# Token block 0 of a two-block layer stack goes ahead from the cross attention to its first expert head

## What is computed

```
h = h + concat([hm, ha]) @ w_out
h = h + memory_cross_attention(rmsnorm(h, g_cross), ...)      # 4 heads of 256, 256 memory rows
xn = rmsnorm(h, g_ffn)
per block of 128 tokens, per head (8 heads), per token:
    q1, q2 = halves of (xn @ w_pq)[head];  s1 = q1 . sub_keys1, s2 = q2 . sub_keys2   # 128 each
    v1, i1 = top_k(s1, 16);  v2, i2 = top_k(s2, 16)
    top_s, pos = top_k(v1[:, None] + v2[None, :], 16);  e = 128 * i1 + i2 at pos
    coef = softmax(top_s) * gelu(expert_down[e] . xn)          # 16 experts
    out += sum over the 16 of coef * expert_up[e]
out = rmsnorm(h + out, g_final)
```

## Time and profile before

| | |
|---|---|
| median of 3 runs | 1639.43 us (1639.33 to 1641.08) |
| profiled execution | 1639.54 us, span 1637.8 us |
| busy: PE, DVE, ACT, POOL | 81%, 59%, 21%, 30% |
| chain that ended last | PE 53%, DMA 26%, DVE 12%, POOL 4% |
| first gather issued | 954.24 us from the span's start |

### The profile page before, as it was taken

How to read it: one execution, slowest core, us unless ns; L and a number is a source line. 1 busy time by engine, 2 the same in 40 slices (tenths; PEclk the granted TensorE clock), 3 DMA queues, 4 the chain that set the end, 5 groups by cost and what they waited for, 6 DMA issues and landing times.

```text
span 1637.8 us, 14570 instructions
## 1 busy us (share of the span) xinstructions
PE 1332.4 (81%) x5214; PEld 936.5 (57%) x5214; DVE 959.0 (59%) x1851; ACT 338.5 (21%) x677; POOL 493.6 (30%) x390
## 2 busy tenths in 40 slices
PE   7999999999999999999999987565566656555554
PEld 5665668888888888886787776222222222222221
DVE  7799974123311000323412168898988998988977
ACT  2444222321100000122312122111111121111111
POOL 2477670000000000000000024755555555555550
PEclk9999999999999999999999998877777777877776
DMA  6222222244344444322242377999999999999995
GB/s 238 77 78 77 78 103 103 103 157 177 128 149 148 150 145 153 128 103 103 77 143 91 117 303 288 405 422 421 422 422 421 422 422 421 422 422 422 421 422 211
DMA packets 55150, 389.75 MB, mean 238 GB/s; under 512 B 6336, under 2 KB 6656, under 8 KB 8368
## 3 DMA queue, kind: packets, MB, share of 16 engines
q0 software_dynamic: 37488, 271.20, 40.1%
...
q10 hardware_dynamic: 1040, 2.26, 0.4%
...
## 4 chain that ended last, share of the span: by engine, by line
PE 53%; DMA 26%; DVE 12%; POOL 4%; issue 2%; ACT 2%; ACTq 0%; DVEq 0%
DMA feat<-in_expert,arena 26%; PE psD L930 16%; PE psD L978 7%; PE psD L384 7%; PE psD L881 6%; POOL feat L1782 4%; PE psD L949 3%; PE psD L1288 1%; DVE feat L1795 1%; PE psN L313 1%; DVE arena L619 1%; DVE feat L1829 1%; DVE feat L537 1%; PE psD L874 1%; PE psD L575 1%
## 5 line engine op out<-in xcount | busy, mean ns | idle before, releaser
L930 PE MATMUL psD<-feat,ring 128*128 128x256 f32 (+1 forms) x1248 | 278.1, 383 | 4.4 <-DVE feat L338 3.2
L930 PEld LDWEIGHTS psD<-feat,ring 128*128 128x128 f32 x1248 | 238.6, 192 | 39.1 <-issue 4.5
L1782 POOL DMA_INDIRECT arena<-in_expert,arena x102 | 140.0, 1373 | 208.7 <-DVE arena L1762 53.0
L1970 POOL DMA_DIRECT2D arena<-in_sub x1 | 0.6, 577 | 525.2 <-ACT feat L1504 525.2
L881 PE MATMUL psD<-feat,ring 128*128 128x256 f32 (+1 forms) x576 | 138.1, 396 | 3.0 <-ACT feat L916 3.0
L1795 DVE CUSTOM_DVE_ANT_0 arena<-arena,feat 128x1024 f32<-128x1024 f32 x102 | 120.7, 1220 | 12.8 <-DMA arena<-in_expert,arena 12.8
L881 PEld LDWEIGHTS psD<-feat,ring 128*128 128x128 f32 x576 | 109.2, 194 | 30.5 <-issue 10.5
L1619 PE MATMUL psB<-arena 128*128 128x512 f32 x96 | 73.2, 923 | 64.1 <-ACT arena L1694 64.1
L1782 POOL DMA_INDIRECT feat<-in_expert,arena x77 | 107.7, 1398 | 57.9 <-DVE feat L1829 17.0
L978 PE MATMUL psD<-feat,ring 128*128 128x256 f32 x512 | 111.2, 379 | 0.0
L384 PE MATMUL psD<-feat,ring 128*128 128x256 f32 x512 | 110.8, 379 | 0.0
...
## 6 DMA issues: line engine op xcount, KB each, us to landing
ring<-in_w SPq DMA_DIRECT2D x108, 1024.0 KB, 4.8
arena<-in_expert,arena POOLq DMA_INDIRECT x102, 27.1
feat<-in_expert,arena POOLq DMA_INDIRECT x77, 28.7
...
arena<-in_w_akv POOLq DMA_DIRECT2D x1, 1024.0 KB, 5.2
feat<-in_memT POOLq DMA_DIRECT2D x1, 1024.0 KB, 5.9
...
ring<-in_expert,arena POOLq DMA_INDIRECT x60, 28.7
```

The costliest lines, as they stand in the source:

```text
L930: mm = nc.tensor.matmul(psD[:, 2 * (c % 2) + m, 0:T], ring[:, c % RING, k, m * P:(m + 1) * P], x[:, k], start=(k == 0), stop=(k == KT - 1))
L1782: (nc.gpsimd.indirect_dma_start(GPAIR[b], None, a["expert"], bass.IndirectOffsetOnAxis(ap=EID[:, t, c:c + 1], axis=0)) .then_inc(s_gb[b], 16))
```

## The change

1. **Sums of squares (norms 2 to 6).** VectorE adds tiles 2, 3 and 4, 5 onto tiles 0, 1 (`squares_dve`); TensorE then has four calls of sums, all after the last chunk or in the middle of the next one, where it had eight.
2. **Cross attention by pairs.** Heads go two at a time for a token block; the scores of a head stand behind the next query chunk.
3. **The output projection is token-major and goes by token block**, adding onto the residual that TensorE puts into PSUM first. ScalarE copies the sum out, squares it and takes the root. Only the gain is applied before the query; the reciprocal root scales the scores and the copy of xn afterwards. Norm 7's own sums are gone.
4. **Block 0 goes ahead**: projection, turn, head 0's queries and scores, and the route come before block 1's. Head 0's query weights are a load of their own (`pq0`) into the room of the squares; the stream has 107 chunks. The residual starts off the accumulator, so TensorE's residual matmuls of the experts go.
5. **Buffers and waits.** `SOON` becomes a list that says which of the sixteen buffers round 0 uses; `LATEWAIT` says what frees each of the others. Buffer 3 (`pq0`'s room) waits for the queries of both blocks.
6. **Order.** The first gelu stands before the seven remaining query chunks, the others behind chunks 1, 4 and 6 of them. Round 1's route comes after round 0's second step instead of before its first; from there the route of a round ends in step 1 of the round before it, half a round later than it did. In the last round `both` comes one step earlier, behind q = 1.

```diff
-SOON = 9
+SOON = [4, 5, 6, 9, 10, 11, 12, 0, 3]
...
-          ("aq", 2), ("mv", 2), ("xva", 3), ("w_out_2", 4), ("xvb", 1), ("xq", 4), ("xo", 4), ("pq", 8)]
+          ("aq", 2), ("mv", 2), ("xva", 3), ("w_out_2", 4), ("xvb", 1), ("xq", 4), ("xo", 4), ("pq", 7)]
...
-    def sums_pe(i, j):
-        nc.tensor.wait_ge(s_sqp, 4 * (i - 2) + j + 1)
-        if j == 0:
-            nc.tensor.wait_ge(s_rt, i)
-        for k in (2 * j, 2 * j + 1):
-            mm = nc.tensor.matmul(psN[:, 0:T2], ones[:, :], SQ[:, k, 0:T2], start=(k == 0), stop=(k == KT - 1))
-        if j == 3:
...
+    def squares_dve(i, link):
+        for j in (1, 2):
+            nc.vector.wait_ge(s_sqp, 4 * (i - 2) + j + 1)
+            ins = nc.vector.tensor_tensor(SQ[:, 0:2, 0:T2], SQ[:, 0:2, 0:T2], SQ[:, 2 * j:2 * j + 2, 0:T2], ALU.add)
+            if j == 1:
+                link(ins)
+        ins.then_inc(s_sqa, 1)
+
+    def sums_pe(i):
+        nc.tensor.wait_ge(s_rt, i)
+        nc.tensor.wait_ge(s_sqa, i - 1)
+        for k in (0, 1, 6, 7):
+            if k == 6:
+                nc.tensor.wait_ge(s_sqp, 4 * (i - 2) + 4)
+            mm = nc.tensor.matmul(psN[:, 0:T2], ones[:, :], SQ[:, k, 0:T2], start=(k == 0), stop=(k == 7))
+        mm.then_inc(s_ms, 1)
...
+    late = {1: slot(feat[:, 3]), 2: slot(ring[:, 3]), 7: slot(ring[:, 0]), 8: slot(ring[:, 1]), 13: slot(ring[:, 2]),
+            14: slot(XN), 15: slot(feat[:, 4])}
+    GPAIR = [soon[SOON.index(i)] if i in SOON else late[i] for i in range(PTOP)]
+    XP = soon[3].rearrange("p (n h s) -> p n h s", n=4, h=2)
+    XPT = soon[4].rearrange("p (n b t) -> p n b t", n=4, b=4)
...
+    def project_pe(t, js, ks):
+        for j in js:
+            c = FIRST["xo"] + j
+            for k in ks:
+                if t == 0 and k == 0:
+                    nc.tensor.wait_ge(s_w[c % RING], (c // RING + 1) * 16)
+                if j == js[0] and k % 4 == 0:
+                    nc.tensor.wait_ge(s_xoc, 2 * t + k // 4 + 1)
+                mm = nc.tensor.matmul(XSUM[t, j // 2][:, (j % 2) * CW:(j % 2) * CW + CW], OX[:, k, blk(t)],
+                                      ring[:, c % RING, k, :], start=False, stop=True, skip_group_check=True)
+            if t:
+                mm.then_inc(s_chunk, 1)
+        if ks[-1] == KT - 1 and js[-1] % 2:
+            mm.then_inc(s_h3, 1) if t == 0 else None
...
+    def blocks_pe():
+        for j in range(4):
+            chunk_pe(FIRST["xq"], j, XN2, T2, fresh=5 if j == 0 else None)
+            if j:
+                cross_scores_pe(j - 1)
+        cross_scores_pe(3)
+        residual_pe(0)
+        cross_turn_pe(0, 0)
+        cross_turn_pe(1, 0)
+        cross_out_pe(0, 0)
+        cross_turn_pe(0, 1)
+        project_pe(0, (0, 1), range(4))
+        cross_out_pe(0, 1)
+        project_pe(0, (2, 3), range(4))
+        project_pe(0, (0, 1), range(4, 8))
+        project_pe(0, (2, 3), range(4, 8))
+        hturn_pe(0, 0)
+        cross_turn_pe(1, 1)
+        hturn_pe(0, 1)
+        nc.tensor.wait_ge(s_sk, 64)
+        query0_pe(0, 0)
+        query0_pe(0, 1)
+        score0_pe(0, 0)
+        cross_out_pe(1, 0)
+        score0_pe(0, 1)
+        xturn_pe(0)
+        cross_out_pe(1, 1)
+        residual_pe(1)
+        project_pe(1, (0, 1), range(8))
+        project_pe(1, (2, 3), range(8))
+        hturn_pe(1, 0)
+        hturn_pe(1, 1)
+        query0_pe(1, 0)
+        query0_pe(1, 1)
+        xturn_pe(1)
+        score0_pe(1, 0)
+        score0_pe(1, 1)
...
+    def blocks_dve(link):
+        for t in range(2):
+            cross_peak_dve(t, 0, link)
+        for t in range(2):
+            cross_share_dve(t, 0, link)
+        for t in range(2):
+            cross_peak_dve(t, 1, link)
+        cross_share_dve(0, 1, link)
+        cross_turned_dve(0, 0)
+        cross_share_dve(1, 1, link)
+        cross_turned_dve(1, 0)
+        cross_turned_dve(0, 1)
+        gains_dve(0)
+        cross_turned_dve(1, 1)
+        gains_dve(1)
+        rstd_dve(0)
...
+    def state_act(t, b):
+        if t:
+            nc.scalar.wait_ge(s_chunk, FIRST["xo"] + 2 * b + 2)
+        else:
+            nc.scalar.wait_ge(s_h3, b + 1)
+        nc.scalar.activation(ACC[:, t, 512 * b:512 * b + 512], XSUM[t, b], ACT.Identity).then_inc(s_acc, 1)
+        if b:
+            nc.scalar.wait_ge(s_acc, 2 * t + 2)
+            nc.scalar.activation(XTOK[:, t], ACC[:, t], ACT.Square, accum_out=F7[:, t, 0:1]).then_inc(s_fsq, 1)
+            nc.scalar.wait_ge(s_fsq, t + 1)
+            (nc.scalar.activation(F7[:, t, 1:2], F7[:, t, 0:1], ACT.Sqrt, bias=epsc[:, 0:1], scale=1.0 / D)
+             .then_inc(s_frt, 1))
...
+    def blocks_act(first_gelu):
+        for j in range(3):
+            pair_act(FIRST["xq"], j, QX[:, 2 * j:2 * j + 2])
+        for t in range(2):
+            cross_exp_act(t, 0)
+        pair_act(FIRST["xq"], 3, QX[:, 6:8])
+        for t in range(2):
+            cross_exp_act(t, 1)
+        nc.scalar.activation(F7[:, 1, 3:4], epsc[:, 0:1], ACT.Sqrt)
+        cross_out_act(0, 0)
+        cross_out_act(0, 1)
+        state_act(0, 0)
+        state_act(0, 1)
+        query0_act(0, 0)
+        query0_act(0, 1)
+        score0_act(0, 0)
+        cross_out_act(1, 0)
+        score0_act(0, 1)
+        xturn_act(0)
+        cross_out_act(1, 1)
+        state_act(1, 0)
+        state_act(1, 1)
+        for b in range(2):
+            nc.scalar.wait_ge(s_ht, 3 + b)
+            for i in range(4):
+                k = 4 * b + i
+                ins = nc.scalar.activation(XN2[:, k, P:T2], HTURN[1, b][:, i * P:(i + 1) * P], ACT.Identity,
+                                           scale=col("g_ffn_2", k))
+            ins.then_inc(s_xh, 1)
+        for m in range(2):
+            query0_act(1, m)
+        first_gelu()
...
     def pair(g, i):
-        return i % SOON if g == 0 else i
+
+        return SOON[i % len(SOON)] if g == 0 else i
...
+        def queries(h):
+            if h == 2:
+                nc.tensor.wait_ge(s_psc, 4)
+            chunk_pe(FIRST["pq"], h - 1, XN2, T2, clear=FIRST["xq"] + 2 + h,
+                     mid=(lambda: scores(h - 1)) if h > 1 else None)
...
-            nc.scalar.wait_ge(s_ps, h + 2)
-            (nc.scalar.activation(SCO[:, :, 2 * h:2 * h + 2], psB[:, h % 2].rearrange("p (t x n) -> p t x n", t=2, x=2),
-                                  ACT.Identity).then_inc(s_psc, 1))
-            if h in (3, 5, 6, 7):
-                coefficients(0, (3, 5, 6, 7).index(h))
+            pair_act(FIRST["pq"], h - 1, QH[:, 2 * h:2 * h + 2])
+            if h > 1:
+                scored(h - 1)
+            if h in (1, 4, 6):
+                coefficients(0, (h + 1) // 2)
+        scored(PH - 1)
...
 
+
...
-
+        last = {}
         for g in range(2 * PH):
             t, h = g // PH, g % PH
             nc.gpsimd.wait_ge(s_eid, g + 1)
             for i in range(PTOP):
                 b = pair(g, i)
-                if g == 0 and i >= SOON:
-                    nc.gpsimd.wait_ge(*used(0, i - SOON))
-                if g == 1 and i < SOON:
-                    nc.gpsimd.wait_ge(*used(0, i + SOON if i + SOON < PTOP else i))
-                if g == 1 and i == SOON:
-                    nc.gpsimd.wait_ge(s_ps, PH + 1)
-                if g > 1:
-                    nc.gpsimd.wait_ge(*used(g - 1, i))
+                if b in last:
+                    nc.gpsimd.wait_ge(*used(*last[b]))
+                elif b == 3:
+                    nc.gpsimd.wait_ge(s_qh, 4)
+                elif g == 0 and i == 0:
+                    nc.gpsimd.wait_ge(s_xo, 4)
+                elif b in LATEWAIT:
+                    nc.gpsimd.wait_ge(*LATEWAIT[b])
+                last[b] = g, i
                 c = h * PTOP + i
...
+    def routes(g, q):
+
+        if g == 0 and q < 2:
+            return []
+        h, part = (g + 1, q + 2) if q < 2 else (g + 2, q - 2)
+        return [(h, part)] if h < 2 * PH else []
...
                 dve.scalar_tensor_tensor(out=ACC[:, t, v], in0=ACC[:, t, v], scalar=FS[:, t, 2:3], in1=GFIN[:, v],
                                          op0=ALU.mult, op1=ALU.mult).then_inc(s_done, 1)
-        for g in range(2):
-            for part in range(4):
-                route_dve(g, part, link)
+        for part in range(4):
+            route_dve(0, part, link)
         for g in range(2 * PH):
             for q in range(len(steps(g))):
                 if g % PH == 0 and q == 0:
                     dve.wait_ge(s_ttc, 2 * (g // PH) + 2)
                 down_dve(g, q)
-                if g + 2 < 2 * PH:
-                    route_dve(g + 2, q, link)
+                if g == q == 0:
+                    rstd_dve(1)
+                for h, part in routes(g, q):
+                    route_dve(h, part, link)
                 if g == 2 * PH - 1 and q == 3:
                     close(1)
                 coef_dve(g, q, link)
                 up_dve(g, q)
+                if g == 0 and q == 1:
+                    for part in range(4):
```

(6 more changed lines are left out.)

362 lines of the change are left out of this document (185 added, 177 removed).

## The result

| | before | after |
|---|---|---|
| median, us | 1639.62 (1639.33 to 1641.08, 4 runs) | 1603.74 (1593.06 to 1609.08, 4 runs) |
| ratio to before | | 0.9766 (95%: 0.974 to 0.9793) |
| profiled execution / its span | 1639.54 / 1637.8 | 1593.06 / 1591.3 |
| first gather | 954.24 | 912.35 |
| first gather to the end of the span | 683.6 | 679.0 |

The change makes the kernel 2.3% faster. Its single times were 1593.06, 1609.08, 1599.22 and 1608.27 us: the profiled execution lies 1.3 us from the predicted 1594.4, and two of the others lie 15 to 16 us above it. The kernel before stays within 2 us. Both facts need an explanation.

The account below looks back on a forecast made before the run. DMA bounds the expert stage, TensorE what precedes it. First gather 912.6 + 1.8 + 653.6 + 2.6 + 0.2 = 1570.8; span 1592.6, forecast 1594 us, 45 faster (chance 0.68, alone 1587 to 1602); range 1586 to 1611.

Parts of the forecast that it names:

- rival 3: Norms 2 to 6: the sums save nothing because VectorE's additions come too late; 9.3 us less gain, 1604 us; chance 0.05.
- the sums of squares: Norms 2 to 6: fewer TensorE calls save 1.73 us each, 2.42 for norm 4, together 9.3 us.
- rival 4: Steady rounds: later addresses let the queue run dry in all 14; at 4 us a round 56 us, 1651; chance 0.03.
- The path of block 0: From the four cross-query chunks to the first gather: 72.2 us instead of 104.5, first gather at 912.6.
- Rival 2: On block 0's path TensorE's clock falls to 1.2 GHz; first gather 21 us later, 1615 us; chance 0.06.
- The four more loads: After the first gather seven query chunks load instead of three: 263 units, four more, costing 9.9 us.
- the slow engine: Expert stage: one DMA engine falls back 0.04 us a unit; 0.2 us for the four more units.
- The start: After the first gather the DMA queue never runs dry; 2.6 us lost, where the kernel before lost 15.2.
- rival 1: After the first gather the start starves as before: 15.2 us lost instead of 2.6, 1607 us; chance 0.14.
- The late addresses: Steady rounds: addresses come half a round later, yet nothing runs dry and rounds stay 40.4 us apart.
- the end: Last round: `both`, 1.23 us, moves ahead of the last landing; gain 1.2 us.
- the 15.2 us: DMA time the kernel before loses after its first gather: 1.1 us until 990 and 14.1 until 1040.

Follow-up runs that it names:

- Experiment 3: The changed kernel with round 0's four gelus back behind query chunks 3, 5, 6 and 7, as in the kernel before: 1615.34 us, ratio 0.9843.
- experiments 6 to 9, 11 and 12: Kernel before, sums change only in norms 2, 4, 6 (1637.18; repeats 11, 12: 1633.13, 1627.35), 3, 5 (1632.38), 4 (1631.71), 2, 6 (1632.47 us).
- experiment 4: The kernel before with only the sums of squares of norms 2 to 6 changed (VectorE adds, four calls instead of eight): 1637.05 us, ratio 0.9979.
- experiment 9: The kernel before with the sums change in norms 2 and 6 only: 1632.47 us.
- experiment 10: The changed kernel with norm 4's sums as before (block 0 ahead, sums change in norms 2, 3, 5 and 6): 1598.02 us, ratio 0.9771.

## Why the prediction was right, and where it was not

**The median, 1603.74,** lies in the stated range and 1.7 us above the 1602 up to which the forecast alone reached. It is also within 0.3 us of rival 3's 1604, which is chance, for rival 3 is refuted. The profiled execution, 1593.06, is the forecast's; what stands above it is told below under the sums of squares. Two slips of the working move nothing: the sum names 0.1 us between the profiled execution and the median and does not take it off, and 44/14, put at 3.2 for rival 4, is 3.1.

**The path of block 0** was right in its size and in every milestone, within 0.4 us. Counting records by measured durations of the same shapes was enough, because TensorE never waited long enough on the way to matter. Rival 2 is out: the granted clock of after is 1.00 in the window over it.

```profile
850.00:1000.00 150.00, 139.85 (x754) 121.18 (x752) 81.62 (x198) 40.18 (x95) 40.72 (x32) 1.00 0.65 266
```

**The four more loads** were to cost 9.9 us. Row 11 of the last round came 657.2 us after the first gather. Less 1.8 until transfers start, 653.6 for 263 units and 0.2 for the slow engine, 1.6 are left for what is lost at the start (predicted 2.6). Without the cost of the four loads that remainder would be 11.5, with a DMA share of 1.00 in all windows. The Trainium skill, "DMA: Bandwidth & Descriptors", section "Issuing engines are not separate DMA queues", was drawn on for this; by that rule, the trace agrees.

**The start** did not starve, for the reason given: ScalarE reaches the gelu at once. Experiment 3 shows that without it rival 1 would have come true and worse, 16.6 us.

**The late addresses and the end** went as predicted: rounds of 40.3 us, and 1591.3 - 1569.54 = 21.8 us behind row 11 instead of 23.05 (predicted 21.85).

**The sums of squares** were right per norm: 1.7 three times and 2.6 for norm 4, where I had reckoned 2.4. The step missed two things that come with the shorter work. First, in each of the twelve traces with new sums in any norm the clock fell to 0.50 for some microseconds in the attention stage, which then took 10.2 to 12.0 us instead of 8.75. In the two traces with all old sums it did not. That costs 1.5 to 3.3 us. Whether the sums decide it or only the moment, the runs do not show, since these two are also the ones in which the stretch began latest: the same two waits, 0.56 or 0.57 and 0.80 or 0.81 us, stand there in all of them. The Trainium skill, "TensorE: Matmul & The Clock Gate", section "Part 1: The HAM clock gate", ties the lower level to a TensorE that has been idle; here it was busy for 5.2 of the 6 us shown above, and without a gap for the 4.9 ahead of the fall, so idleness in that plain sense is not what the trace has. Second, norm 4's change brings the upper level of times, in a third of the runs. That is where the working fell short: beside the calls saved it put nothing in the sum. Of the 9.7 us between the median and my 1594 the upper level is the larger part: two of the four runs of after lay there, and the other two have a median of 1596.1. The median is inside the range, but the range was made wide for a starving start, and not for this.

**How much of the gain is real.** The term that I took from one execution and should not have is the 15.2 us that the kernel before loses at its start. In the traces of experiments 6 to 9, 11 and 12, which have before's order there, the tenth gather comes 24.3 us after the first and the end 677.9 to 678.2 us after it, while the profile of before has 29.1 and 683.6, and experiment 4's 31.9 and 686.0. The difference is in TensorE's query chunks behind the first gather. ScalarE's copy of the first chunk there and TensorE's scores of the same head, of before and then of experiment 9 (first gathers at 954.24 and 952.16):

```profile
965.63 0.60 ACT L1094 ACTIVATE feat<-psD 128x512 f32<-128x512 f32 x1 [9.43 <-remote]
...
966.37 1.13 PE L1601 MATMUL psB<-arena,feat 128*128 128x128 f32 x8 [3.90 <-issue]
```

```profile
960.43 0.60 ACT L1129 ACTIVATE feat<-psD 128x512 f32<-128x512 f32 x1 [6.31 <-PE psD L965]
...
961.17 1.13 PE L1636 MATMUL psB<-arena,feat 128*128 128x128 f32 x8 [0.78 <-ACT feat L1129]
```

At +12.1 us in one and +9.0 in the other. The chunk's own records take 7.07 us in both, but in before the copy starts 3.1 us after the last of them (962.47), in experiment 9 at once (960.39). What held up TensorE's signal there, the trace does not show. The chunk behind the wait then took 8.76 us instead of 7.07 (granted clock 0.87 from 960 to 970 us), and the two together are the 4.8 us by which the tenth gather is later (29.1 against 24.3). ScalarE's gelu stood behind these chunks before the change, so their delay became the gathers' delay. So against a start without that delay, the stage behind the first gather is 1 us longer after the change, not 4.6 shorter: 9.9 for the loads, against 7.9 no longer lost (9.5 there by the same books, 1.6 now) and 1.3 at the end. The path ahead of it was long in the profile of before, too: from norm 6's root to the first gather it has 107.87 us, the seven other traces with before's order 105.32 to 107.62, so that the 32.0 us gained there are 29.5 to 31.8 against those. This fits the two groups in which before ran at 1636, where block 0 alone gained 30.2 and the change without norm 4's part 37.9, and the group and profile in which it ran at 1639 to 1643 and lower runs of the whole change gained 44 to 46.5. I have no trace of the kernel before itself from the 1636 groups, so this last link is argued and not shown.

**A steadier version.** Block 0 ahead with norm 4's sums left on TensorE (experiment 10) gives up 2.6 us of every run and has none of the upper runs. Its five runs spread over 2.6 us. It was not run beside the changed kernel itself, so which median is lower is not measured; by these numbers they are about even, a third of 11 us against 2.6.
